# A second norm's root applied behind the projections: a two-block transformer kernel on one core

## What is computed

```python
def rmsnorm(x, gain):
    x32 = x.astype(jnp.float32)
    y = x32 * lax.rsqrt(jnp.mean(x32 * x32, axis=-1, keepdims=True) + RMS_EPS)
    return (y * gain.astype(jnp.float32)).astype(x.dtype)

def conv_glu_ffn(xn, w_up, conv_w, conv_b, w_down):
    gu = xn @ w_up
    gate, up = jnp.split(gu, 2, axis=-1)
    gate = causal_dwconv(gate, conv_w) + conv_b.astype(gate.dtype)
    return (jax.nn.silu(gate) * up) @ w_down

    # first block, for each of its three parts
    h = conv_glu_ffn(rmsnorm(x, norm_ffn_pre[l]), w_ffn_in[l], ffn_conv_w[l], ffn_conv_b[l], w_ffn_out[l])
    x = x + rmsnorm(h, norm_ffn_post[l])
```

## Time and profile before

| | us |
|---|---|
| median of 3 runs | 1563.71 (1563.61 to 1568.01) |
| profiled execution, device time | 1567.91 |
| its span in the profile | 1566.0 |
| TensorE busy | 1491.3 (95%) |
| VectorE busy | 1146.3 (73%) |
| ScalarE busy | 838.1 (54%) |

### The profile page before, as it was taken

How to read it: one execution, slowest core, us unless ns; L and a number is a source line. 1 busy time by engine, 2 the same in 40 slices (tenths; PEclk the granted TensorE clock), 3 DMA queues, 4 the chain that set the end, 5 groups by cost and what they waited for, 6 DMA issues and landing times.

```text
span 1566.0 us, 30024 instructions
## 1 busy us (share of the span) xinstructions
PE 1491.3 (95%) x10194; PEld 1378.2 (88%) x10194; DVE 1146.3 (73%) x2152; ACT 838.1 (54%) x1174; POOL 19.0 (1%) x25
## 2 busy tenths in 40 slices
PE   7998977999989999998999999999999999999998
PEld 6887966999869999878999999999988888889997
DVE  5767655788655566665499999999888888876665
ACT  7634555544456466654577666777633433334443
POOL 0000000000003000000000000000000000000000
PEclk9999988999999999999999999999999999999999
DMA  6452441555644532254476776444477777766553
GB/s 271 137 172 76 151 145 55 186 181 181 207 135 155 178 126 82 81 189 164 157 223 219 216 222 203 136 139 144 154 251 244 238 243 240 240 206 203 187 185 139
DMA packets 97494, 276.41 MB, mean 177 GB/s; under 512 B 10760, under 2 KB 37256, under 8 KB 96908
## 3 DMA queue, kind: packets, MB, share of 16 engines
q1 hardware_dynamic: 65664, 240.54, 47.2%
q10 hardware_dynamic: 31756, 34.88, 6.3%
HBM read 260.16 MB, written 16.26 MB: 177 GB/s over the span
## 4 chain that ended last, share of the span: by engine, by line
PE 81%; DVE 9%; ACT 5%; issue 2%; DMA 1%; PEld 0%; ACTq 0%; DVEq 0%; PEldq 0%
PE acc L1150 7%; PE acc L1154 7%; PE acc L1153 7%; PE ring L545 7%; PE ring L548 6%; PE ring L549 6%; PE acc L1072 5%; PE acc L1076 5%; PE acc L1077 5%; PE ring L1114 4%; PE acc L545 3%; PE acc L548 3%; PE acc L549 3%; DVE sb_halves L1728 3%; PE ring L1137 2%
## 5 line engine op out<-in xcount | busy, mean ns | idle before, releaser
L1728 DVE TENSOR_TENSOR sb_halves<-sb_raw,sb_halves 128x1024 fp32r<-128x1024 f32 x450 | 546.4, 1229 | 193.0 <-ACT sb_halves L1218 189.6
L1218 ACT ACTIVATE sb_halves<-sb_raw 128x1024 fp32r<-128x1024 f32 x450 | 469.7, 1058 | 316.0 <-PE acc L1150 167.3
L1072 PE MATMUL acc<-sb_XH,sb_halves 128*128 128x256 f32 x800 | 232.8, 291 | 4.6 <-ACT sb_early L1542 4.4
L545 PE MATMUL ring<-sb_XH,sb_halves 128*128 128x256 f32 x784 | 224.7, 287 | 3.1 <-DVE sb_halves L1728 3.1
L1077 PE MATMUL acc<-sb_XH,sb_halves 128*128 128x256 f32 x800 | 226.1, 283 | 0.0
L1076 PE MATMUL acc<-sb_XL,sb_halves 128*128 128x256 f32 x800 | 226.1, 283 | 0.0
L548 PE MATMUL ring<-sb_XL,sb_halves 128*128 128x256 f32 x784 | 223.5, 285 | 0.0
L549 PE MATMUL ring<-sb_XH,sb_halves 128*128 128x256 f32 x784 | 223.3, 285 | 0.0
L1150 PE MATMUL acc<-sb_halves,sb_coefh 128*128 128x512 f32 x512 | 200.3, 391 | 2.0 <-DVE sb_coefl L2278 2.0
L1153 PE MATMUL acc<-sb_halves,sb_coefh 128*128 128x512 f32 x512 | 200.0, 391 | 0.0
L1154 PE MATMUL acc<-sb_halves,sb_coefl 128*128 128x512 f32 x512 | 199.9, 390 | 0.0
(11 more groups left out here) (335 smaller groups left out, 2532.6 us busy)
## 6 DMA issues: line engine op xcount, KB each, us to landing
sb_raw<-wstream SPq DMA_DIRECT2D x450, 512.0 KB, 3.6
ahead<-sb_early ACTq DMA_DIRECT2D x100, 128.0 KB, 2.5
sb_area<-ahead ACTq DMA_DIRECT2D x98, 128.0 KB, 3.4
sb_area<-gains ACTq DMA_DIRECT2D x4, 512.0 KB, 4.4
sb_area<-consts SPq DMA_DIRECT2D x1, 1782.0 KB, 13.4
sb_area<-mem ACTq DMA_DIRECT2D x1, 1024.0 KB, 11.4
relvec<-relrow ACTq DMA_DIRECT2D x1, 1024.0 KB
sb_area<-keys ACTq DMA_DIRECT2D x1, 1024.0 KB, 5.5
```

The lines of the kernel that those rows point to most:

```text
L545: ins = mm(out, w[0], x[0], start=first, stop=False)
L1072: ins = mm(o, w[0], XH[:, c, :], start=c == 0, stop=False)
L1218: A(hi[:, r, :], raw[:, r, :], ACT.Copy).then_inc(S("hi_ready"), 1)
L1728: tt(lo[:, r, :], raw[:, r, :], hi[:, r, :].bitcast(F32), ALU.subtract).then_inc(S("lo_ready"), 1)
```

## The change

At the four boundaries k = 2 to 5 the projection is made from x times the gain, without the root:

- `proj_acc` signals each accumulation bank; the squares and the gain product go by bank, and the mean of the first bank (`half_mean`) is the bias of the root. The residual is added in halves, and each signals `x_half`.
- `tile_T` turns the unscaled x by tile and half; that of tile 0 is called inside `proj_acc` ahead of the last piece of tile 1. `tile_XH` and `tile_XL` write 128-column parts. VectorE's weight remainder for piece 1 of the next slot stands between the residual of tile 1 and `tile_XL`.
- `proj_unscaled` takes two ring banks for the first slot, runs all products with the high part of x first, and then those with `XL`. Its second piece frees in the second pass.
- The squares of x and their root (`x_root`) come behind `tile_XH` on ScalarE, `x_inverse` gives `rstd_x`; `spread_roots`, `root_row` (two transposes into `acc`) and `turned_roots` give `root_T`, the row of roots.
- Cross queries: the root and P ** -0.5 scale the scores (`rstd_q`). Feed-forward: both halves are multiplied by `root_T`, the gate one slot later than before, and the rounding to `hidh` moves from VectorE to ScalarE. Second mixer: copies move from ScalarE to VectorE with `root_T`; values, merge gates and scores ps take a column scale on ScalarE, in two instructions where there was one; the decays follow slot 2.
- Queries pq use own tiles `UH`, `UL`; `xs` = (UH + UL) times the roots, split into `XH`, `XL` for the experts.
- `root_ready` (which loads the table for the root) moves: before `feed(("mix", 2))`, before `joint_roots(2)`, before the feeds of down, behind `feed(("wout", 3))`. Gain loads and the xkeep store move behind `tile_XH` and `x_root`.

```diff
             def joint(use, key):
+                    at = 4 * (use - 1) + 2 * t
+                    dve.wait_ge(S("acc_squared"), at + 1)
+                    link(tt(tmp[:, 0:512], acc[:, t, 0, :], gain[:, 0:512], ALU.mult))
+                    link(ts(half_mean[:, t:t + 1], sbank[:, 2 * t:2 * t + 1], 1.0 / DM, EPS, ALU.mult, ALU.add), "half_mean")
+                    dve.wait_ge(S("acc_squared"), at + 2)
+                    link(tt(tmp[:, 512:DM], acc[:, t, 1, :], gain[:, 512:DM], ALU.mult), "acc_free")
                     inverse(t, rms)
-                    link(stt(out=x[:, t, :], in0=tmp, scalar=rstd[:, t:t + 1], in1=x[:, t, :], op0=ALU.mult, op1=ALU.add),
-                         "resid" if t else "resid_first")
-                    if t == 0:
-                        feed(key)
-                    normed_tile(x, rms_x, t)
+                    for h in range(2):
+                        half = slice(h * 512, (h + 1) * 512)
+                        link(stt(out=x[:, t, half], in0=tmp[:, half], scalar=rstd[:, t:t + 1], in1=x[:, t, half],
+                                 op0=ALU.mult, op1=ALU.add), "x_half")
+                    remainder(2 * SLOT_AT[key] + 2 + t, (2 * SLOT_AT[key] + 2 + t) % NR)
...
         def _(act):
-            for f in range(FC + 1):
+            feed(("up", 0))
+            for t in range(NT):
+                x_root(3, t)
+            for f in range(1, FC + 2):
                 if f < FC:
                     feed(("up", f))
-                    b = got(act, ("up", f))
-                    link(A(gpad[:, f % 2, 2:258], b[:, 0:T], ACT.Copy), "ff_gate")
-                if f:
+                if f <= FC:
                     act.wait_ge(S("ff_conv"), f)
                     g = (f - 1) % 2
                     link(A(fa[:, g, :], fa[:, g, :], ACT.Silu), "ff_silu")
+                if f >= 2:
+                    act.wait_ge(S("ff_prod"), f - 1)
+                    link(A(hidh[:, f - 2, :], ht[:, f % 2, :], ACT.Copy), "ff_hid")
+            root_ready()
             for i in range(FC // 2 - 1):
                 feed(("down", i))
...
         def _(dve):
+            for f in range(1, FC + 3):
+                if 1 < f < FC:
                     feed(("up", f))
...
+                if f <= FC:
+                    g = f - 1
+                    o, p = fa[:, g % 2, :], gpad[:, g % 2, :]
+                    link(tt(p[:, 2:258], got(dve, ("up", g))[:, 0:T], root_T, ALU.mult), "dve_step" if g else "ffn_gate")
+                    link(ts(o, p[:, 0:256], C("fconv", g), C("fb", g), ALU.mult, ALU.add))
+                    link(stt(out=o, in0=p[:, 1:257], scalar=C("fconv", 22 + g), in1=o, op0=ALU.mult, op1=ALU.add))
+                    link(stt(out=o, in0=p[:, 2:258], scalar=C("fconv", 44 + g), in1=o, op0=ALU.mult, op1=ALU.add),
                          "ff_conv")
...
+                if 2 <= f <= FC + 1:
+                    g = f - 2
+                    dve.wait_ge(S("ff_silu"), g + 1)
+                    b = got(dve, ("up", g) if g else ("up", 0, 1))
+                    link(tt(ht[:, g % 2, :], fa[:, g % 2, :], b[:, T:2 * T] if g else b[:, 0:T], ALU.mult), "ffn_up")
+                    link(tt(ht[:, g % 2, :], ht[:, g % 2, :], root_T, ALU.mult), "ff_prod")
+                if f >= 3:
+                    g = f - 3
+                    dve.wait_ge(S("ff_hid"), g + 1)
+                    link(tt(hidl[:, g, :], ht[:, g % 2, :], hidh[:, g, :].bitcast(F32), ALU.subtract), "ffn_hidden")
...
```

More of the change, by code:

```diff
@@ L186, in attention, with norm @@
                 job(("ysT", 1), "ysT_ready")
-    def norm(k):
-        for c in range(4):
-            job(("xn", k, c), "xT_ready")
+    def norm(k, t=None):
+        for c in range(4) if t is None else range(2):
+            job(("xn", k, c) if t is None else ("xn", k, t, c), "xT_ready")
     norm(0)
@@ L227, in jobs @@
     job(("yT", 1), "yT_ready")
-    norm(2)
-    for i in range(2):
-        job(("cq", i), "cq_copied")
+    norm(2, 0)
+    norm(2, 1)
+    job(("cq", 0), "cq_copied")
+    job(("cq", 0, 1), "cq_copied")
+    job(("cq", 1), "cq_copied")
     attention(ATT2, len(ATT1))
     job(("coT", 1), "coT_ready")
[L233 to L236, removed]
+    norm(3, 0)
+    norm(3, 1)
+    job(("up", 0), "ffn_gate")
+    job(("up", 0, 1), "ffn_up")
+    job(("up", 1), "ffn_up")
+    for f in range(2, FC):
+        job(("up", f), "ffn_up")
+    norm(4, 0)
+    norm(4, 1)
     for i in range(7):
@@ L1447, in _ @@
             joint_roots(3, ("down", FC // 2 - 1))
-            norm_T(4, "g_mix2")
+            tile_XH(4, "g_mix2", XH)
+            for t in range(NT):
+                x_root(4, t)
             T2 = [("fq", 0), ("fq", 1), ("fk", 0), ("fk", 1), ("nq", 0), ("nq", 1), ("kk",)]
@@ L2024, in _ @@
             joint(1, ("mix", 3))
-            rest_norm(2, "g_cross")
-            for i in range(2):
-                feed(("cq", i))
+            tile_XL(2, "g_cross", (XH, XL))
+            feed(("cq", 0))
+            x_inverse()
+            link(ts(rstd_q, rstd_x, P ** -0.5, None, ALU.mult))
+            feed(("cq", 1))
             take(("co", 1), 0)
@@ L2313, in _ @@
             for t in range(NT):
-                dve.wait_ge(S("acc_ready"), NT * 6 + t + 1)
-                link(tt(x[:, t, :], x[:, t, :], accf[:, t, :], ALU.add), "resid" if t else "resid_first")
+                for h in range(2):
+                    half = slice(h * 512, (h + 1) * 512)
+                    dve.wait_ge(S("acc_ready"), 4 * 6 + 2 * t + h + 1)
+                    link(tt(x[:, t, half], x[:, t, half], acc[:, t, h, :], ALU.add), "x_half")
             dve.wait_ge(S("ld_gain"), 64)
```

350 lines of the change are left out of this document (243 added, 107 removed).

## The result

The changed kernel takes 1584.05 us, the median of 4 runs (1582.46 to 1585.53), against 1565.13 for the kernel before in the same comparison (4 runs, 1563.61 to 1568.01): the ratio is 1.0121, with a 95% interval of 1.0104 to 1.0138. That is 18.9 us slower (16 to 22 by the interval), where +22.2 was forecast and 1586.0 as the time. The profiled execution took 1582.46, the lowest of the four, with a span of 1580.6.

What follows compares the result with a forecast made beforehand. TensorE, busy 95%, was taken as the bound, so only its waits matter. Terms -7.6 + 1.0 + 18.4 + 7.2 + 2.2 + 0.75 + 0.3 = +22.2 us gave 1586; range 1567 to 1596.

Steps and rivals of the forecast that it cites:

- The ring: Feed-forward up slots: ScalarE and VectorE waiting on each other, 6.73 us a turn against 5.76, +18.4 over 19 turns.
- Rival (a): Feed-forward: the mutual wait doesn't bind since VectorE's busy sum 5.58 fits; not slower, 1560 us; chance 0.11.
- Rival (b): Feed-forward: hand-overs overlap, a turn near 6.2 us, 8.5 instead of 18.4, total 1576; chance 0.12.
- rival (c): Up slots: the clock falls in each slot's new gaps, +29 us, total 1615; chance 0.05.
- The entry: Start of the feed-forward loop: first Silu, with table load, comes late after the root row, which waits for slot 1; +1.0.
- The stop: Start of the down projection: TensorE stands 7.4 us after two pieces, against 0.2 before; +7.2.
- The clock's restart: Down projection after TensorE's idle gap: 3.6 to 5.5 us at half rate, +2.2 (0 to 2.8).
- The rule on table loads: Skill's rule of about 1.38 us drain beside each 1.28 table load; would add 1.4 at down, left out.
- The boundaries: Four norm boundaries: shorter gaps, 8.5 us against 10.06 at three and 6.0 against 8.47 at the fourth.
- The last residual: Final residual add, done by halves: gains 0.5 us.
- Restarts at the boundaries: Low clock after the four norm gaps: as before, no gain.
- the root rows: Three pairs of added transposes on TensorE, 0.25 us each: +0.75.

Runs made afterwards that it cites:

- the later waits: Changed kernel with ScalarE's Silu and hidden rounding one iteration later; 1561.58 us, ratio 0.9963 to the kernel before.
- the kernel with the boundaries' remainder moved as well: Changed kernel with later Silu and hidden copy, root row behind down casts, first down piece earlier, boundary weight remainder behind XL's first half; 1552.35 us, ratio 0.9905.

## Why the prediction was right

**The ring** was the largest term and right in kind, place and number: 6.73 forecast for a turn, 6.80 measured, 19 turns, 19.8 us instead of 18.4. The 0.07 are hand-overs: the sum had one of 0.10 and one of 0.03, the trace has two of 0.10, from VectorE to ScalarE and back. Rival (a), that it doesn't bind because busy time fits, fell with the experiments: busy time did fit, at 5.76 with the later waits, and the order of waits cost 1.04 on top. Rival (b) wanted a turn of 6.2, and rival (c) a lower clock in the slots, where it stayed at 1.00.

**The entry** of 1.0 did not occur. The forecast had Silu's table load behind the wait for the first convolution. ScalarE's timeline shows it ahead of that wait:

```profile
273.04 1.28 ACT L1533 ACT_TABLE_LOAD   x1
280.16 0.42 ACT L1533 ACTIVATE sb_area<-sb_area 128x256 f32<-128x256 f32 x1 [5.84 <-DVE sb_area L2185]
```

**The stop** at down was forecast at 7.4 and took 7.24; its net of the 0.21 before is 7.0. The root row's share of it, 1.52, is shown. The clock's restart cost 1.8 (half of 3.6), where 2.2 stood.

*The rule on table loads.* In the stop the load begins at 421.34, takes 1.28, and the root starts at 422.63, 0.01 behind its end. The Trainium skill (ScalarE: Activation LUTs, What ACT_TABLE_LOAD costs) would have some 1.38 us of drain beside it; the trace does not show it here either.

**The boundaries** gained 8.4 (1.9, 1.8, 1.87, 2.8) where 7.1 of the 7.6 stood for them. The 8.5 and 6.0 that were to be read from last to first product hold the moved transposes, which lie ahead of the last product; without them they are 7.5 and 5.0, against 7.40 and 4.86 measured. Ahead of the second mixer the links are 0.49 to the second Square, 0.69 for it and its read, 1.08 for gain half and reciprocal, 1.58 for the residual halves, 1.17 for the remainder, 2.29 for the eight remainders of XL and 0.10 to the first product, which waits for the last of the eight. The terms that were over-sized are those groups, 2.5 in the sum, and the transposes inside the accumulation, 0.79 and not 0.97, as they run at full clock there; the residual halves were under-sized by 0.2. The last residual gave 0.4 of its 0.5.

**Restarts at the boundaries** were put at no gain. From the first product to the rise of the clock it took 5.6, 3.0, 5.5 and 3.6 us before, and 5.7, 4.9, 3.7 and 5.5 after. Half of the differences is 0.0, +0.95, -0.9 and +0.95, in all +1.0, which was not in the sum.

**Together**: 19.8 + 7.0 + 1.8 - 8.4 - 0.4 + 1.0 + 0.75 for the root rows (from their count, as forecast) - 2.4 for the pitch = 19.1, against 18.9 measured by the medians. The forecast of 22.2 stood above it by the pitch (2.4), the boundaries and last residual (1.2), the entry (1.0) and the stop, restart and rest (0.9), and below by the ring (1.4) and the restarts at the boundaries (1.0): the largest miss of the sum is the pitch, a term that it did not have.

That 19.1 and 18.9 agree so closely is luck. The terms are read from two executions that lie 14.6 us apart, and the sum leaves out what else differs between them. The experts' products waited 1.2 us less in the changed kernel. And the kernel before was at the low clock for three further stretches of 3.4 us, from 14.9, 158.3 and 1127.7, at a cost of up to 1.7 each; the changed kernel waited 1.1 at 26.8 for a weight remainder, which the kernel before did not. With these the sum is 13.9, for 14.6. The last of the three, TensorE alone, before and after (us, busy, clock, DMA share, GB/s):

```profile
1127.70:1131.00 3.30, 3.30 (x9) 0.50 0.72 213
```

```profile
1144.40:1147.70 3.30, 3.30 (x16) 1.00 0.70 221
```

Both follow the same wait of 2.02 us, at 1127.09 and at 1143.80, and only one of them brought the low clock. Single executions of one kernel differ by such falls, so a term of a few us is safe only where it is read at its own place.

What stays open: what picks between the paces 0.1133 and 0.1178, whether the longer time at the low clock in the kernel with the boundaries' remainder moved as well is more than scatter, and how the 512-column products of the last stage depend on distance.

## What to carry to other kernels

When work moves between two engines that each run in program order, write down one turn of the waits, start to start, with the work queued behind each wait, and compare it with the slot; the busy sums say only whether it could fit. Such a ring is cut for nothing by asking for last iteration's result instead of this one's, if a buffer is there to hold it. A piece of 0.45 us cost its full length in the ring and nothing beside it. At a drain, see what comes before the first cast of the next stage, above all a table load.

## What the runs showed of the hardware

**The pitch of matmuls depends on where the two operands lie.** Products of 256 columns with 128x128 weights started 0.1200 us apart at full granted clock where the distance between streamed and weight tile was 0 modulo 512 bytes, in all kernels, and 0.1133 or 0.1178 apart where it was 64 or 448. Moving XH and XL by 448 bytes and the tiles behind them by 512 was worth 12 us by the medians, 8.5 by the ratios. The Trainium skill (SBUF — State Buffer, Who interferes with whom) lists TensorE's two reads, operand and weights, as independent; by that the pitch would not change. The rows say otherwise, and the measurement decides. Only three distances were run, and one placing shows both faster paces, so the pattern is shown in part and its mechanism isn't.

**A table load can run ahead of its activation's wait.** It ran at 273.04, the activation at 280.16 after 5.84 us of waiting, so it was free there. This is not so everywhere: at 584.40 in the same kernel the load itself came 1.5 us behind the instruction ahead of it, with the activation 0.01 behind its end.

**Idle time spread through the slots left the clock alone.** In the up slots TensorE was busy 87.76 of 100 us, in pieces with gaps of 0.8, and the granted clock stayed at 1.00; idle times of 7.24, and of 2.80 and 2.58 with transposes between, were followed by 0.50. A wait of 2.02 was followed by 0.50 in the kernel before (1127.09) and not in the changed one (1143.80). At the stop and the four boundaries of the changed kernel the clock rose 3.6 to 5.7 us behind the first product.
